# Sixteen sliding-window attention heads in a two-block transformer kernel: the product of probabilities and values turned round

## The reference

```
s_band = jnp.einsum('bqhgd,bkhd->bhgqk', qi, kb) * scale          # masked to |qpos - kpos| <= 128
s_meta = jnp.einsum('bqhgd,bmhd->bhgqm', qi, k_meta) * scale
p = jax.nn.softmax(jnp.concatenate([s_band, s_meta, s_sink], axis=-1), axis=-1)
o = einsum('bhgqk,bkhd->bqhgd', p_band, vb) + einsum('bhgqm,bmhd->bqhgd', p_meta, v_meta)
merged = g_swa * (o_swa @ w_branch_swa) + g_diff * (o_diff @ w_branch_diff)
```

## Time and profile before

| | value |
|---|---|
| median of 3 runs | 894.6 us (894.13 to 897.55) |
| the profiled execution | 891.72 us, its span 889.5 us |
| PE busy | 835.5 us, 94% of the span |
| DVE, ACT, POOL busy | 552.0 us (62%), 471.8 us (53%), 127.4 us (14%) |
| mean granted clock of PE | 0.987 |
| DMA | 138.12 MB, 155 GB/s |
| the four swa groups' attention | from 393 to about 488 us of the span |

### The profile page before, as it was taken

The page is one execution under the profiler, slowest core; times in us unless marked ns, Lnnn a source line. Parts: engine busy times, 40 slices in busy tenths (PEclk is TensorE's granted clock), DMA queues, the critical chain, the costliest instruction groups (busy, mean ns, idle before and its releaser), DMA issues.

```text
span 889.5 us, 13103 instructions
## 1 busy us (share of the span) xinstructions
PE 835.5 (94%) x4390; PEld 692.9 (78%) x4390; DVE 552.0 (62%) x849; ACT 471.8 (53%) x962; POOL 127.4 (14%) x197
## 2 busy tenths in 40 slices
PE   7799999999999998889989999999998999999995
PEld 5578878778887875789878888888886788888884
DVE  5476667675765768756555765766575655455453
ACT  5475655365565547646555565555535544344343
POOL 0200121000011105663222334200000000000000
PEclk9999999999999999999999999999999899999999
DMA  9944444365633448852212434456654556656641
GB/s 277 259 143 119 145 123 139 121 191 150 179 98 117 138 126 264 261 157 79 73 47 71 126 110 139 143 159 195 215 189 143 178 183 197 208 159 194 210 140 47
DMA packets 147583, 138.12 MB, mean 155 GB/s; under 512 B 15184, under 2 KB 115680, under 8 KB 147520
## 3 DMA queue, kind: packets, MB, share of 16 engines
q1 hardware_dynamic: 145440, 130.21, 48.3%
q0 software_dynamic: 2080, 7.09, 2.8%
HBM read 136.22 MB, written 1.05 MB: 154 GB/s over the span
## 4 chain that ended last, share of the span: by engine, by line
PE 55%; ACT 6%; DVE 4%; issue 2%; DMA 1%; POOL 1%; ACTq 0%; DVEq 0%; POOLq 0%
PE psum L1026 45%; PE psum L1005 5%; PE psum L1108 3%; PE psum L1218 2%; ACT w_hi L1260 2%; ACT probs L1372 2%; DMA raw<-in_w_in 1%; DVE w_lo L1427 1%; DVE stats L1537 1%; ACT xn L1282 1%; PE psum L1221 1%; ACT gtmp L1402 0%; DVE xn L1466 0%; DVE x L1470 0%; POOL stage L979 0%
## 5 line engine op out<-in xcount | busy, mean ns | idle before, releaser
L1427 DVE TENSOR_TENSOR w_lo<-raw,w_hi 128x1024 fp32r<-128x1024 f32 (+1 forms) x254 | 298.8, 1193 | 143.5 <-ACT w_hi L1260 86.1
L1260 ACT ACTIVATE w_hi<-raw 128x1024 fp32r<-128x1024 f32 (+1 forms) x254 | 253.4, 1016 | 79.0 <-PE psum L1026 50.5
L1026 PE MATMUL psum<-w_hi,h_hi 128*128 128x512 f32 (+1 forms) x656 | 261.3, 398 | 7.4 <-DVE h_lo L1476 4.9
L1026 PE MATMUL psum<-w_lo,h_hi 128*128 128x512 f32 (+1 forms) x656 | 247.7, 378 | 0.0
L1026 PE MATMUL psum<-w_hi,h_lo 128*128 128x512 f32 (+1 forms) x656 | 247.2, 377 | 0.0
L1026 PEld LDWEIGHTS psum<-w_hi,h_hi 128*128 128x128 f32 x656 | 124.9, 190 | 29.5 <-issue 9.8
L1026 PEld LDWEIGHTS psum<-w_lo,h_hi 128*128 128x128 f32 x656 | 124.3, 189 | 19.5
L1026 PEld LDWEIGHTS psum<-w_hi,h_lo 128*128 128x128 f32 x656 | 125.0, 190 | 15.8
L1372 ACT ACTIVATE probs<-psum,stats 128x272 f32<-128x272 f32 (+2 forms) x104 | 47.7, 468 | 87.5 <-DVE stats L1529 31.8
L1026 PE MATMUL psum<-w_hi,m_hi 128*128 128x512 f32 x192 | 76.5, 398 | 8.6 <-ACT w_hi L1260 4.5
L1026 PE MATMUL psum<-w_lo,m_hi 128*128 128x512 f32 x192 | 75.0, 391 | 0.0
(11 more groups left out here) (150 smaller groups left out, 1027.5 us busy)
## 6 DMA issues: line engine op xcount, KB each, us to landing
raw<-in_w_in SPq DMA_DIRECT2D x112, 256.0 KB, 3.5
raw<-in_w_in SPq DMA_DIRECT2D x44, 512.0 KB, 4.3
raw<-in_w_ffn_in SPq DMA_DIRECT2D x88, 256.0 KB, 3.9
raw<-in_w_out SPq DMA_DIRECT2D x24, 512.0 KB, 3.3
raw<-in_w_in SPq DMA_DIRECT2D x64, 192.0 KB, 2.7
raw<-in_w_ffn_out SPq DMA_DIRECT2D x22, 512.0 KB, 4.6
raw<-in_w_mem_kv SPq DMA_DIRECT2D x8, 512.0 KB, 3.8
raw<-in_w_branch_swa SPq DMA_DIRECT2D x8, 512.0 KB, 3.4
```

The lines of the kernel that those rows point to most:

```text
L1026: last = nc.tensor.matmul(psum[:, bank, 0:n], sx[name][:, c, t * P:(t + 1) * P], wx[:, u["slot"], kk, 0:n], start=u["first"] and kk == 0 a ...
L1260: nc.scalar.activation(w_hi[:, u["slot"], :, 0:n], raw[:, u["raw"], :, 0:n], ACT.Copy)\
L1427: nc.vector.tensor_tensor(w_lo[:, u["slot"], :, 0:n], raw[:, u["raw"], :, 0:n], w_hi[:, u["slot"], :, 0:n].bitcast(F32), ALU.subtract)\
```

## The change

The value product of the swa heads is turned round. The values (64 columns) become stationary and the probabilities move (256 columns, both token tiles at once), so that the output comes out transposed and needs no `turn_mix`. Two heads of a pair write the upper and lower 64 partitions of one PSUM bank, from the two column halves of the array. As queries now lie along the columns of the output, the softmax's reciprocal can't be applied there; a new step `scale` multiplies the probabilities of a pair by it before they are turned. The meta columns of a pair are turned by a step of their own, `turn_tm`, into a ring bank. `out_t` replaces `out` and `turn_mix`: ACT copies its 128x256 result to `mix_hi` and DVE subtracts `mix_lo`. The maximum and the sink operations on DVE are done for a pair at once.

```
-    "swa": dict(turn_qk=(3.25, 2.75), scores=(4.5, 4.5, 6.5, 6.5), turn_p=(5.5, 6, 7.5, 8),
-                out=(6.25, 7, 8.25, 9), turn_mix=(10.5,)),
+    "swa": dict(turn_qk=(3.25, 2.75), scores=(4.5, 4.5, 6.5, 6.5), scale=(6.5, 8.5), turn_p=(7, 7.25, 9, 9.25),
+                turn_tm=(7.25, 9.25), out_t=(8.25, 10.25)),
...
+        elif what == "scale":
+            s["scaled"] = pl.next("scales")
+            for h in s["heads"]:
+                h["scaled"] = s["scaled"]
+        elif what == "turn_tm":
+            s["batch"] = pl.next("batches") - 1
+            s["tm"] = pl.next("tms")
+            ring(s, ("tm_ready", s["tm"]))
...
+        elif what == "out_t":
+            s["o"] = pl.next("outs") - 1
+            s["hi"] = pl.next("his")
+            s["turned"] = pl.next("turns")
+            ring(s, ("turned", s["turned"]), "out_")
+            g["last_out"] = s["o"] + 1
+            outs_of_pt.extend([s["o"] + 1] * 2)
...
+                    elif kind == "swa":
+                        pe.wait_ge(scaled, s["scaled"])
...
+                elif what == "turn_tm":
+                    wait(pe, s["bank_free"])
+                    pe.wait_ge(scaled, s["scaled"])
+                    turn([(psum[0:META, s["bank"], (2 * n + t) * P:(2 * n + t + 1) * P],
+                           probs[:, h["j"] % 4, t, T:T + META], P)
+                          for n, h in enumerate(s["heads"]) for t in range(NT)])
+                elif what == "out_t":
...
+                    keys = [(vs[:, kt, v0:v0 + DH], p_t, slice(kt * T, (kt + 1) * T)) for kt in range(NT)]
+                    keys.append((gflat[:, META_VA + g["kv"] * DH:META_VA + (g["kv"] + 1) * DH], p_tm, slice(0, T)))
+                    for n, (value, prob, at) in enumerate(keys):
+
+                        for i, h in enumerate(s["heads"]):
+                            last = nc.tensor.matmul(psum[DH * i:DH * (i + 1), s["out_bank"], 0:T], value,
+                                                    prob[:, h["pt"] % 2, at], start=(n == 0), stop=(n == 2),
+                                                    skip_group_check=True)
+                    last.then_inc(out_done, 1)
...
+                elif what == "turn_tm":
+                    act.wait_ge(tp_done, s["batch"] + 1)
...
+                    nc.scalar.activation(p_tm[0:META].rearrange("p n q -> p (n q)"), psum[0:META, s["bank"], :],
+                                         ACT.Copy).then_inc(tm_ready, 1)
+                elif what == "out_t":
+                    act.wait_ge(out_done, s["o"] + 1)
+                    wait(act, s["dest_free"])
+                    name, c = s["g"]["mix"][s["c"]]
+                    nc.scalar.activation(S_hi[name][:, c, :], psum[:, s["out_bank"], 0:T], ACT.Copy)\
+                        .then_inc(turned_hi, 1)
...
+                    if kind == "swa":
+                        if "mate" not in s:
+                            continue
+                        dve.wait_ge(scores_done, j + 2)
...
+                        link(nc.vector.tensor_reduce(
+                            two[:, :, 0:2],
+                            psum[:, 2:6, 0:T + META].rearrange("p (h t) k -> p h t k", h=2), AX.X, ALU.max, negate=True))
...
+                elif what == "scale":
+                    j = s["heads"][0]["j"]
+                    dve.wait_ge(probs_ready, j + 2)
+                    two, inv = stats[:, j % 4:j % 4 + 2], rec[:, j % 4:j % 4 + 2, 0:NT]
+                    link(nc.vector.tensor_tensor(two[:, :, 2:4], two[:, :, 2:4], two[:, :, 6:8], ALU.add))
+                    link(nc.vector.reciprocal(inv, two[:, :, 2:4]))
+                    pr = probs[:, j % 4:j % 4 + 2]
+                    nc.vector.tensor_tensor(pr, pr, inv.unsqueeze(3).to_broadcast([P, 2, NT, T + META]), ALU.mult)\
+                        .then_inc(scaled, 1)
+                elif what == "out_t":
+                    dve.wait_ge(turned_hi, s["hi"])
+                    name, c = s["g"]["mix"][s["c"]]
+                    nc.vector.tensor_tensor(S_lo[name][:, c, :], psum[:, s["out_bank"], 0:T],
+                                            S_hi[name][:, c, :].bitcast(F32), ALU.subtract).then_inc(turned, 1)
...
-                        if kind == "swa":
-                            link(nc.vector.tensor_tensor(stats[:, j % 4, 2:4], stats[:, j % 4, 2:4],
-                                                         stats[:, j % 4, 6:8], ALU.add))
...
-                    elif kind == "swa":
-                        for t in range(NT):
-                            last = nc.vector.tensor_scalar(st[:, t, a * DH:(a + 1) * DH],
-                                                           psum[:, s["out_bank"], t * DH:(t + 1) * DH],
-                                                           rec[:, j % 4, t:t + 1], None, ALU.mult)
```

More of the change, by code:

```diff
@@ L168, in attention_slots @@
         jobs[a]["mate"] = jobs[a + 1]
+    pairs = [dict(g=g, c=n, heads=(jobs[2 * n], jobs[2 * n + 1])) for n in range(2)]
     for what, places in SLOTS[g["kind"]].items():
@@ L176, in attention_slots @@
                 s = dict(g=g)
+            elif what in ("scale", "turn_tm", "out_t"):
+                s = pairs[n]
             else:
@@ L740, in build @@
         gates_ready = sem("gates_ready")
+        scaled = sem("scaled")
+        tm_ready = sem("tm_ready")
         meta_padded = sem("meta_padded")
@@ L755, in build @@
                    out_done=out_done, blended=blended, s_mem=s_mem, turned=turned, out_used=out_used,
-                   pt_ready=pt_ready)
+                   pt_ready=pt_ready, tm_ready=tm_ready)
         def wait(eng, what):
@@ L841, in build, with mixed_before @@
         by_ga = {g["ga"]: g for g in pl.groups if "ga" in g}
+        def mixed_before(ga):
+            last = [g["mixed"] for g in by_ga.values() if g["ga"] < ga and g["ga"] % 2 == ga % 2 and "mixed" in g]
+            return max(last)
         ffn = [g for g in pl.groups if g["kind"] == "ffn"]
@@ L1189, in _ @@
                     turn(todo)
+                elif what == "turn_tm":
[5 more added lines that the diff above has]
+                elif what == "out_t":
+                    g = s["g"]
+                    vs = stage[:, g["ga"] % NSTAGE]
+                    v0 = KINDS["swa"]["v"]
+                    pe.wait_ge(pt_ready, s["heads"][1]["pt"] + 1)
+                    pe.wait_ge(tm_ready, s["tm"])
+                    wait(pe, s["out_bank_free"])
+                    keys = [(vs[:, kt, v0:v0 + DH], p_t, slice(kt * T, (kt + 1) * T)) for kt in range(NT)]
[6 more added lines that the diff above has]
+                    last.then_inc(out_done, 1)
+                    for t in range(NT):
+                        where[g["mix"][s["c"]] + (t,)] = s["turned"]
                 elif what == "out":
@@ L1390, in _ @@
                     last = nc.scalar.activation(p_t[:, s["pt"] % 2, 0:n], psum[:, s["bank"], 0:n], ACT.Copy)
-                    if kind in ("swa", "diff"):
+                    if kind == "diff":
                         b0 = 2 + 2 * (s["j"] % 2)
```

51 lines of the change are left out of this document (31 added, 20 removed).

## The result

The changed kernel took 908.0 us (median of 4 runs, 904.6 to 910.2), the kernel before 895.7 in the same session (894.1 to 897.6): a ratio of 1.013, 95% interval 1.009 to 1.018. It is slower by 12.3 us, as forecast in its sign; 902.5 was predicted, and 908.0 lies in the range of 888 to 911, at the upper end of the forecast's own (897 to 908). The profiled execution took 904.64 us, its span is 902.9. Both profiled executions are at the fast end of their runs.

What follows compares the result with a forecast made beforehand. PE's own work, alternating with a chain PE, DVE, ACT, DVE, PE, was taken as the limit. PE's work -9.4, old waits -7.2 and new waits +25.3 gave +8.7 us; forecast 902.5 us, range 888 to 911, its own 897 to 908.

Steps and rivals of the forecast that it cites:

- PE's work: swa stage: turned value products save 7.7 us and dropped output turns 1.8, so PE's work falls by 9.4 us.
- The scores' factor of 0.61: Overlap of row halves in the scores, applied to a pair's value product: 2.60 x 0.61 = 1.6 us.
- Rival 2: Column halves don't overlap fully: 910.5 us if serial, 907.6 if only weight loads stay in the open; chance 0.20.
- W1: After a group's second scores, PE waits for DVE's maximum, sink operations and product before turning probabilities: 2.35 us, four times, 9.4.
- W2: PE's next q or second head's turn waits for ACT's copies: 0.75 in two groups, 1.2 and 0.25 in the third; 2.95 us.
- W3: After a group's first value product, the small turn waits for ACT's copy of turned probabilities: 3.0, 3.75, 3.75; 10.5 us.
- W4: Behind the first diff scores, two maxima and the product precede PE's next turn, then a bank wait: 2.45 us.
- Old waits: PE's existing idle stretches in the swa stage, 7.2 us, were to go because turns no longer wait for o_st.
- Clock: PE's fall to half clock in the swa stage: one kept; none would be -1.8 us, four +5.
- The signs: Stage waits under 16 us or a pair over 2 us would refute it; swa0's second scores end near 401.
- Rival 1: PE's saving wins if new waits stay at today's 7.2 us: 883 to 885 us; chance 0.12.
- The product beside POOL: DVE's eight 1088-column products slowed by POOL's rope beside some of them: at most 8 x 0.16 = 1.3 us.

Runs made afterwards that it cites:

- e6: The changed kernel with all swa steps' places spread by durations from the traces, turns and value products later: 880.0 us, 0.982 of the kernel before.
- e7: The changed kernel without the 1088-column product of probabilities and reciprocals, sums and reciprocals still made: 897.2 us, 1.002 of the kernel before.
- e5: The changed kernel with only the swa turns of probabilities and the value products moved one place later: 888.8 us, 0.991 of the kernel before.
- e4: The changed kernel with the first pair's 1088-column product moved ahead of the second pair's maximum on DVE: 919.0 us, 1.025 of the kernel before.

## Why the prediction was right, point by point

The order of things was right: PE's saving, the two links that make PE wait and where they lie, and the sign. That the size came out so near is in part luck, since two errors cancel: the waits were forecast 2.9 us too long, and the clock's cost was left out of the sum.

- **PE's work: right in the sum, partly by luck.** I had -9.4 us. The account gives 109.5 less 1.5 for before's one fall (an estimate by e6's price), 108.0, and 104.4 - 5.5 = 98.9 after: -9.1. A pair takes 1.46 us, predicted 1.6, so by my own terms it should have been 8 x 1.10 + 1.8 = 10.6; 1.5 us of that didn't come, and no run says where. The serial price of 0.217 us for a record was exact: it is the pace within each half. The scores' factor of 0.61 was the wrong form: the two halves overlap fully and a fixed 0.15 us is added. For the scores, 4 x 0.23 + 0.2 = 1.12 gives the same 0.61.
- **Rival 2 fell.** The rule of the Trainium skill ("TensorE: Matmul & The Clock Gate", "Part 3: Packing small matmuls — row/col tiling"), that a weight load overlaps with a running matmul only across row groups, doesn't hold here: loads of 136 ns for halves that share all rows left the records 0.217 us apart. The prediction says that no run shows it yet, but the trace of before did. A unit tile's six matmuls take 1.05 us, 0.175 each, and each brings a weight load over all 128 rows that takes longer than that (its mean of 190 ns stands behind the busy time):
```profile
L1026 PEld LDWEIGHTS psum<-w_hi,h_hi 128*128 128x128 f32 x656 | 124.9, 190 | 29.5 <-issue 9.8
```
- **W1: right.** Four waits, predicted 2.35 each, 9.4 in all; measured 2.92, 2.07, 2.07 and 1.92, 9.0. e7 shows that the product is in them: 1.60, 0.75, 0.72 and 0.59 are left without it.
- **W2: too high.** Predicted 2.95 in all; in the third group one wait of 0.99 and one of 0.34 behind it appeared, for 1.2 and 0.25. The two of 0.75 didn't.
- **W3: right in kind, too high in size.** Predicted 3.0, 3.75, 3.75; measured 2.20, 2.93, 2.93, 8.1 instead of 10.5. In the one shown, the copy that PE waits for is ready 7.8 us behind the value product's end (predicted 7.4 + 0.74), and PE came to it after 4.9 us, not 4.5.
- **W4: 1.89 for 2.45. Old waits: not all gone.** In the first group the second scores wait 1.20 us for the first pair's exponentials, and two turns wait 0.45 and 0.17 for the product, which the walk didn't have. Together PE is idle for 15.2 us more; I had 25.3 - 7.2 = 18.1.
- **Clock: the step that failed.** I kept one fall and put four of them, +5, in the bounds only. There were three, one of them twice as long as the others: 13.6 us at half clock instead of 3.4, worth 4.0 us. Waits of 2 to 3 us in a row were the point of my own walk; I should have carried a fall behind some of them into the forecast.
- **Sum:** -9.1 + 15.2 + 4.0 = +10.1 us in the stage, against +8.7. With the clock as forecast it would have been +6.1. In the profiled pair the other 3.4 us lie ahead of the stage, in instructions that the change doesn't touch; the forecast had nothing for them.
- **The signs.** The pair's 1.46 us and PE's 23.1 us of idle time are on the right side of what I had called wrong (over 2, under 16). swa0's second scores end at 405.14; less the 3.4 us from ahead of the stage that is 401.7, where 401 was forecast. The first diff scores start at 493.75, later than 484.
- **Rival 1** (PE's saving wins) is what e5 and e6 are: it said that the change turns to a gain once new waits are below 16.6 us, and that nothing forces product and turn to stand so close. With 9.9 and 4.9 us of idle time in the stage both are gains.
- **The product beside POOL: real and small.** Seven of the eight products take 1.29 us. The eighth starts while a POOL operation (L1012) runs, and has POOL's last copy of the rope behind it:
```profile
420.25 1.67 DVE L1636 TENSOR_TENSOR probs<-probs,rec 128x1088 f32<-128x1088 f32 x1
...
419.91 0.86 POOL L1012 TENSOR_TENSOR stage<-rtmp 128x320 f32<-128x320 f32 x1
420.84 1.24 POOL L1018 COPY stage<-stage 128x128 f32<-128x128 f32 x1
```
L1012 runs for another 0.52 us behind the product's start, and the product takes 0.38 longer than the others. The copy takes 0.29 us alone; here it ends 0.16 behind the product's end. So each of the two waited for the one in front of it, which agrees with the rule that the prediction quotes. The eight together lost 0.4 us on DVE; I had allowed 1.3.

## What to carry to other kernels

Work cut from the busiest engine saves its time only if that engine doesn't wait instead. Count the chain from what a step needs to the step itself, over all engines, with the weight splits and copies of other work that stand in it, and hold it against the busiest engine's own work in between. When a change adds a link to that chain, move its consumer later in the same edit; here this turned +12 us into -16. And price idle stretches of PE above their length, since the clock falls behind some of them: 17 us more at half clock cost e4 7.8 us for the same instructions.

## What the runs showed of the hardware that I had not expected

- Two 64-column halves of the array, with different weights and different moving data and all 128 rows in common, run beside each other at full pace: 1.46 us for twelve records that take 2.60 one by one. PE also begins a half's next work while the other half still runs, when the program has them one after the other (1.94 us).
- With the same work in the stage, PE's busy time was 98.9 (e6, with its five records), 100.6, 104.4, 110.3 and 112.2 us at mean clocks of 1.00, 0.98, 0.95, 0.91 and 0.89. The traces of the last four have 3.4, 13.6, 23.9 and 30.7 us at half clock in the stage, so a stretch costs between 0.4 and 0.5 of its length.
- Not each wait brings a fall. In the change the clock went down at 408.82, within the wait that ends at 409.55, and at 436.13 and 477.09, just behind those that end at 435.53 and 476.72. It stayed up behind those that end at 426.39, 451.57, 460.73 and 487.72, though the one before 451.57 is as long (2.93 us) as the one before 476.72.
- A product of DVE that reads and writes SBUF and POOL's operations wait for each other. The copy above took four times its time. In e6 four of the eight products start while a POOL operation runs, by 0.2 to 0.5 us, and take 1.37, 1.37, 1.69 and 1.69 us instead of 1.29; the POOL operation behind each ends only behind the product.
